# Stick scores and first-branch scores as one group in the middle of the third chunk

## The reference

```python
(qa, ka, va, qi, ki, wi, qf, kf, vf, fg, qs, ks_, vs, gates) = split(x @ w_in)
o_a = dsa_attention(qa, ka, va, ...)        # softmax over 64 selected keys, distance bias
o_b = forgetting_attention(qf, kf, vf, ...) # softmax with a cumulative forget bias
# stick breaking, per head: z = qs ks^T / 8, strict: key < query
log_beta = log_sigmoid(z)
log_one_minus = where(strict, log_sigmoid(-z), 0)
later = reverse_cumsum(log_one_minus) - log_one_minus
o_c = where(strict, exp(log_beta + later), 0) @ vs
```

## Time and profile before

| | us |
|---|---|
| median of 3 runs | 1392.6 |
| lowest and highest run | 1392.53, 1392.9 |
| the profiled execution | 1392.8 |
| its span in the trace | 1391.1 |
| TensorE busy in it | 1371.2 |
| VectorE busy | 1023.4 |
| ScalarE busy | 798.4 |

### The profile page before, as it was taken

How to read it: one execution, slowest core, us unless ns; L and a number is a source line. 1 busy time by engine, 2 the same in 40 slices (tenths; PEclk the granted TensorE clock), 3 DMA queues, 4 the chain that set the end, 5 groups by cost and what they waited for, 6 DMA issues and landing times.

```text
span 1391.1 us, 25268 instructions
## 1 busy us (share of the span) xinstructions
PE 1371.2 (99%) x9114; PEld 1242.2 (89%) x9114; DVE 1023.4 (74%) x1595; ACT 798.4 (57%) x1306; POOL 23.4 (2%) x71
## 2 busy tenths in 40 slices
PE   8999999999999999999999999999999999999998
PEld 8999999988888878888899989989989898888887
DVE  5786776677666686666778888888888876666665
ACT  4444554644334354444668898898898843544443
POOL 6000000000000000000000000000000000000000
PEclk9999999999999999999999999999999999999999
DMA  8565554556555736655564444535435276566661
GB/s 265 147 190 145 143 158 151 184 182 200 193 181 185 232 116 210 196 181 181 153 182 130 129 120 132 141 104 151 135 96 153 78 195 211 151 200 198 196 193 61
DMA packets 298383, 227.82 MB, mean 164 GB/s; under 512 B 10882, under 2 KB 280404, under 8 KB 298324
## 3 DMA queue, kind: packets, MB, share of 16 engines
q1 hardware_dynamic: 298324, 227.01, 54.9%
HBM read 225.90 MB, written 1.08 MB: 163 GB/s over the span
## 4 chain that ended last, share of the span: by engine, by line
PE 90%; DVE 5%; ACT 2%; DVEq 2%; issue 1%; ACTq 0%; POOL 0%; POOLq 0%
PE G L1960 7%; PE G L1961 7%; PE G L1962 7%; PE M L1977 7%; PE M L1965 7%; PE M L1966 7%; PE G L1977 7%; PE M L1967 7%; PE G L1979 3%; PE M L1979 3%; PE G L2683 2%; PE G L2080 2%; PE G L1965 2%; PE G L1967 2%; PE G L1966 2%; PE M L2521 1%
## 5 line engine op out<-in xcount | busy, mean ns | idle before, releaser
L1151 DVE TENSOR_TENSOR w_lo<-w_raw,w_hi 128x2048 fp32r<-128x2048 f32 (+2 forms) x249 | 480.9, 1935 | 156.7 <-ACT w_hi L622 153.8
L622 ACT ACTIVATE w_hi<-w_raw 128x2048 fp32r<-128x2048 f32 x198 | 377.8, 1909 | 174.6 <-PE G L1962 75.0
L1960 PE MATMUL G<-xa,w_hi 128*128 128x256 f32 x992 | 297.4, 300 | 0.0
L1962 PE MATMUL G<-xa,w_lo 128*128 128x256 f32 x992 | 280.4, 283 | 0.0
L1961 PE MATMUL G<-xa,w_hi 128*128 128x256 f32 x992 | 280.2, 282 | 0.0
L1960 PEld LDWEIGHTS G<-xa,w_hi 128*128 128x128 f32 x992 | 189.5, 191 | 4.9 <-issue 4.2
L1961 PEld LDWEIGHTS G<-xa,w_hi 128*128 128x128 f32 x992 | 189.5, 191 | 1.7 <-issue 1.7
L1962 PEld LDWEIGHTS G<-xa,w_lo 128*128 128x128 f32 x992 | 189.0, 191 | 0.0
L1965 PE MATMUL M<-w_hi,xb 128*128 128x512 f32 x304 | 119.0, 391 | 0.6 <-DVE xb L1151 0.5
L1966 PE MATMUL M<-w_lo,xb 128*128 128x512 f32 x304 | 118.7, 390 | 0.0
L1967 PE MATMUL M<-w_hi,xb 128*128 128x512 f32 x304 | 118.3, 389 | 0.0
(11 more groups left out here) (400 smaller groups left out, 2518.6 us busy)
## 6 DMA issues: line engine op xcount, KB each, us to landing
w_raw<-in_w_in SPq DMA_DIRECT2D x150, 512.0 KB, 4.8
w_raw<-in_ffn_w_in SPq DMA_DIRECT2D x88, 512.0 KB, 5.0
w_raw<-in_w_ff SPq DMA_DIRECT2D x64, 512.0 KB, 4.4
w_raw<-in_ffn_w_out SPq DMA_DIRECT2D x44, 512.0 KB, 4.8
w_raw<-in_w_in SPq DMA_DIRECT2D x33, 256.0 KB, 3.3
w_raw<-in_w_out SPq DMA_DIRECT2D x16, 512.0 KB, 4.1
w_raw<-in_w_branch_gdn SPq DMA_DIRECT2D x16, 512.0 KB, 5.2
w_raw<-in_w_branch SPq DMA_DIRECT2D x12, 512.0 KB, 4.2
```

The source lines that it names most:

```text
L622: nc.scalar.activation(w_hi[:, slot, :], w_raw[:, slot, :], ACT.Copy).then_inc(hi_ready, 1)
L1151: return v.tensor_tensor(dst, src, hi.bitcast(F32), ALU.subtract)
L1960: mm(out_, w[0], x[0], start=first, stop=False)
L1962: return mm(out_, w[1], x[0], start=False, stop=last_)
```

## The change

On TensorE the stick scores and the first branch's scores, with their waits, become one group. It runs as the `between` of chunk 2, that is after 24 of its 48 products. Ahead of it stand chunk 0, chunk 1 and the first half of chunk 2 without a group in between; behind it the second half of chunk 2 and chunk 3. No other engine's code changes.

```diff
-        with pe.Fori(0, PAIRS) as p:
-            pair_chunk(0, p, col_gemm)
-            pair_chunk(1, p, col_gemm)
+        def first_scores(p):
             copied(0, p)
             pe.wait_ge(ol_ready[2], p + 1)
             for e in range(2):
...
                 mm(M[:, 4 + e, 0:T], ks_t[lo_:lo_ + HD, 0:P], qs_t[lo_:lo_ + HD, :], start=True, stop=True)
                 ins = mm(M[:, 4 + e, T:3 * P], ks_t[lo_:lo_ + HD, P:T], qs_t[lo_:lo_ + HD, P:T], start=True, stop=True)
             ins.then_inc(z_done, 1)
-            pair_chunk(2, p, col_gemm)
             copied(1, p)
             pe.wait_ge(ol_ready[0], p + 1)
             scores(0, 0, qa_t, ka_t, p)
+
+        with pe.Fori(0, PAIRS) as p:
+            pair_chunk(0, p, col_gemm)
+            pair_chunk(1, p, col_gemm)
+            pair_chunk(2, p, lambda slot, bank: col_gemm(slot, bank, between=lambda: first_scores(p)))
             pair_chunk(3, p, tok_gemm)
```

## The result

The changed kernel takes 1402.51 us (median of 4 executions, 1401.76 to 1404.00), the kernel before 1392.75: a ratio of 1.0071, with a 95% interval of 1.0059 to 1.0083. It is 9.8 us slower. The sign was forecast, the size was not: 7.6 us were, and the median lies 0.3 us above the top of the range. The profiled execution is the slowest of the four, 1404.0, with a span of 1402.3 and a mean granted clock of 0.997, where the kernel before has 0.999. Two executions of the later runs, 6591.5 us in y4 and 1675.6 us of the kernel before, lie far outside all others and are left out of the ratios.

What follows compares the result with a forecast made beforehand. TensorE was taken as full, with no slack in the stick chain. A delay of 1.90 us per pair, 4 x 1.90 = 7.6, without subtracting the merged group's 0.40, gave 1400.2 us; range 1397.6 to 1402.2.

Steps and rivals of the forecast that it cites:

- the chain: Stick scores, ScalarE, VectorE, stick values in each pair: claimed to have no slack, a tenth of a microsecond before TensorE's load.
- Part 1: TensorE's two score sets as one group: 0.40 us less per pair, 1.6 in all, bounds 0 and 0.69.
- the prediction's lower bound: Saving of 0 from the merged group, if the two waits between its sets hold the weight loads back.
- Parts 2 and 3: Stick scores half a chunk later: ScalarE's Abs starts 1.92 us later, and the delay passes down VectorE to L1349's end.
- Part 4: First branch's scores about 3 us earlier on TensorE: worth nothing, since their reader on VectorE is late anyway.
- rival C: TensorE's clock falls to 1.2 GHz after its idle times: one chunk per pair 5.8 us dearer, about 1423 us; 3%.
- the sign "a granted clock under 1.00": A granted clock under 1.00 in the changed kernel's profile would show the forecast wrong.
- A: Not slower: the stick chain has hidden slack, only the merged group's 0.40 us per pair counts, 1391.0 us; 4%.
- B: Partly absorbed: VectorE catches up the 0.52 us idle before L1337 in each pair, 1398.1 us; 5%.

Runs made afterwards that it cites:

- y4: Changed kernel with three small identity products on TensorE filling only the wait for stick_ready: 1400.42 us against 1392.65 for the kernel before, ratio 1.0056.
- x6: Changed kernel with the whole merged group another half chunk later, behind chunk 2: 1412.12 us against 1392.70 for the kernel before, ratio 1.0146.
- x5: Changed kernel with VectorE's low weight half for the next pair's first chunk moved behind the second normalisation: 1391.57 us against 1392.70 for the kernel before.
- y1: x1 with VectorE's low weight half for the next pair's first chunk moved behind the second normalisation: 1392.07 us against 1392.65 for the kernel before.
- z1: x1 with VectorE's weight half that waits for chunk 2's end moved directly behind the row maximum: 1392.11 us against 1392.73 for the kernel before.
- x4: Changed kernel with small identity products on TensorE ahead of both waits, first branch's values and stick_ready: 1399.89 us against 1392.58 for the kernel before.
- x3: Kernel before with only the first branch's scores moved, into the middle of chunk 2: 1396.36 us against 1392.58, ratio 1.0027.
- y3: Changed kernel with four small identity products filling only the wait ahead of the first branch's values: 1400.12 us against 1392.65 for the kernel before.
- x1: Changed kernel with the merged group directly behind chunk 1 instead of mid chunk 2: 1395.81 us against 1392.58 for the kernel before, ratio 1.0023.
- x7: Changed kernel with the merged group after 6 of chunk 2's 48 products: 1395.16 us against 1392.70 for the kernel before, ratio 1.0017.

## Why the prediction was wrong

**What bounds the kernel, and the chain: right.** The tenth of a microsecond between L1349 and the load that needs it was not even slack: in the changed kernel, where TensorE does wait, the load comes at 119.48, 0.12 behind L1349's end at 119.36, and in the kernel before it was 0.13. x6 shows that each further microsecond passes through, and x5 that 2.7 us off the chain end the loss.

**Part 1: mechanism right, size a little off.** The merged group saves 0.29 per pair (x5), not 0.40. TensorE's timeline of the changed kernel around it, which answers to the earlier trace rows together:

```profile
96.73 0.28 PE L1962 MATMUL G<-xa,w_lo 128*128 128x256 f32 x1
96.94 0.71 PE L2225 MATMUL M<-arena 64*128 64x256 f32 x4
...
97.70 0.49 PE L2202 MATMUL M<-arena 64*128 64x128 f32 x4
97.92 0.70 PE L2203 MATMUL M<-arena 64*128 64x256 f32 x4
...
98.78 0.28 PE L1961 MATMUL G<-xa,w_hi 128*128 128x256 f32 x1
```

The group takes from 96.85 to 98.66, 1.81 us, where the two took 2.10 and 1.70 was forecast. As forecast, none of the saving shows in the changed kernel's time. Directly behind chunk 1 the group saves only 0.12: a pair of y1 or z1 lasts 43.30 us. There the second set's weight load has to wait for the copy of chunk 1, as the prediction's lower bound feared; in y1:

```profile
94.83 0.31 PEld L2202 LDWEIGHTS M<-arena 64*128 64x128 f32 x4 [0.18 <-DVE arena L1281]
```

**Parts 2 and 3, and their sum: right.** Abs 1.94 later (97.93 - 0.4 against 95.59; forecast 1.92), L1349 1.95 (1.92), the waits 1.09 and 0.87 (1.2 and 0.9), a pair at full clock 1.92 longer. So this part is 4 x 1.92 = 7.7 us; 7.6 was forecast. In x4, whose clock stayed up and whose pairs are 45.25 to 45.28 us, 1399.89 - 1392.58 = 7.3 are left.

**Part 4: the reason was wrong, though nothing of it shows.** "Worth nothing" looked only at who reads the first branch's scores. Their move also pushes back the end of chunk 2, on which ScalarE's split and VectorE's half wait. In the changed kernel the stick scores' larger delay hides it (L1151 starts there at 104.97 without idle time); alone, in x3, it costs 3.8 us.

**The clock is the step that failed.** The sum gave it nothing behind the two idle times that it forecast, and rival C, which named it, had 3%. I took the first 5.00 us of the program, idle at a granted clock of 1.00, as evidence that gaps do not bring the clock down here. They say nothing about a gap in the middle of a stream. The runs showed a fall to half clock behind the idle times of 1.09 and 0.87 us, 1.50 us each, in two pairs of four, so 3.0 us in the profiled execution. With the gaps filled (x4, y3, y4) the falls and 2 to 4 us are gone. C's mechanism was right and its size was not: one chunk per pair at half pace, 5.8 us, in all four pairs. Its price was put beside the forecast as a separate case of 1423 us, when it is a term that adds to it: 7.6 plus none, one or two falls of some 1.5 us would have been 1400.2 to 1403.2 and would have held the result.

The range came within 0.3 us of the result by luck. Its upper end had 0.5 us per pair for a restart of TensorE's stream, and no run shows that: a pair at full clock grew by 1.92, where 1.90 was forecast. And the sign "a granted clock under 1.00" could not have told anything as it stood, since the kernel before has a mean of 0.999.

The Trainium skill (TensorE: Matmul & The Clock Gate, section "Why this matters for your kernels") warns of idle gaps between bursts of matmuls only when they are longer than any in these pairs. The traces differ from it: the clock fell behind gaps of 1.09 and 0.87 us, and in x6 behind one of 2.22. The measurement decides.

**Rivals A and B**: A is refuted by the result, 9.8 us slower, and by x6 and x5. B's absorption of the 0.52 us is refuted by the rows of L692 and L1290: the exponentials start 0.03 behind L1286, whose end is 108.54 + 0.68, and L1290 comes 1.90 behind their start in both traces, so the idle time that vanished at L1337 came back at L1290.

## What to carry to other kernels

An engine without idle time may still be a tenth of a microsecond from waiting: before a group is moved on it, compare the end of every step that it waits for with the start of its wait, and follow both what the moved results release and what the work that is pushed back releases (here the ring slot of a chunk). A move that makes TensorE wait needs a second term, for the clock, added to the wait's own price, unless a later wait takes it up, as in x6. The remedy is on the other engines' queues: work that nobody needs yet, placed behind the chain and not in it.

## What had not been expected

- The granted clock fell behind two idle times of 1.09 and 0.87 us with 1.75 us between their ends, in two of the four pairs; with one idle time of that size per pair (0.7 in x1, x3 and x7, 0.8 in y3, 1.1 in y4) it stayed at 0.999 or above. But x6 shows it fall behind a single one of 2.22. Why some pairs and not others (one and three in one trace, two and four in another) stays open.
- A fall costs 1.50 us in the changed kernel: the products come at half pace only over a stretch of some 3 to 4 us, of which half is work that is done in any case, and not over a whole chunk. In x6 the same stretch costs nothing, because TensorE would have waited in any case.
